# A hybrid encoder step: the order and banks of the last output stage, its last tile in halves, and a wait of the recurrence's tanh

## The reference

```
layer 0:  h = rms_norm(x) * (1 + scale) + shift;  u = h @ w_in        (x_a, g_a, q, k, v, g_b)
          y_a = rg_lru(conv(x_a)) * silu(g_a)     # r, i = sigmoid(xc @ w_a), sigmoid(xc @ w_x)
          y_b = window_attention(q, k, v) * silu(g_b)
          x = x + gate * rms_norm([y_a, y_b] @ w_out)
layer 1:  h = ...;  u = h @ w_in;  q, k, v = silu(conv(.));  gated delta rule over 8 heads
          x = x + gate * rms_norm((rms_norm(o) * silu(z)) @ w_out)    # the last stage
```

## Time and profile before

| | us |
|---|---|
| median of 3 runs (lowest, highest) | 1477.13 (1476.96, 1477.85) |
| the profiled execution | 1476.26 |
| its span, first to last instruction | 1474.5 |
| TensorE busy | 1418.5 (96%) |
| VectorE busy | 760.1 (52%) |
| ScalarE busy | 409.0 (28%) |
| GpSimd busy | 174.4 (12%) |
| TensorE's granted clock, mean share of full speed | 0.995 |

### The profile page before, as it was taken

How to read it: one execution, slowest core, us unless ns; L and a number is a source line. 1 busy time by engine, 2 the same in 40 slices (tenths; PEclk the granted TensorE clock), 3 DMA queues, 4 the chain that set the end, 5 groups by cost and what they waited for, 6 DMA issues and landing times.

```text
span 1474.5 us, 29798 instructions
## 1 busy us (share of the span) xinstructions
PE 1418.5 (96%) x12752; PEld 891.1 (60%) x12752; DVE 760.1 (52%) x1765; ACT 409.0 (28%) x1009; POOL 174.4 (12%) x341
## 2 busy tenths in 40 slices
PE   5999999999999999899999999999999999999997
PEld 3577765666644545566666666666666666665533
DVE  4737872444332444745747557465474574742252
ACT  5124431444411324112213123132221321322110
POOL 1122200000000110110201112011020020100120
PEclk9999999999999999999999999999999999999999
DMA  9520016000256011210111111101111011030151
GB/s 372 205 67 4 33 64 249 0 1 0 104 198 237 36 57 24 77 33 31 47 47 43 35 40 52 44 33 48 32 60 34 29 47 33 22 135 1 45 171 57
DMA packets 54439, 105.02 MB, mean 71 GB/s; under 512 B 34490, under 2 KB 37378, under 8 KB 51474
## 3 DMA queue, kind: packets, MB, share of 16 engines
q1 hardware_dynamic: 54308, 103.13, 20.2%
HBM read 88.25 MB, written 14.86 MB: 70 GB/s over the span
## 4 chain that ended last, share of the span: by engine, by line
PE 63%; DVE 6%; issue 1%; ACT 1%; DMA 0%; POOL 0%; POOLq 0%; DVEq 0%; ACTq 0%; SPq 0%
PE psum L787 61%; PE psum L790 2%; DVE mem L2228 1%; DVE mem L2245 1%; DVE mem L2460 1%; DVE mem L2259 1%; ACT mem L1644 0%; DVE mem L2397 0%; DVE mem L2238 0%; DVE mem L2406 0%; DVE mem L2142 0%; DMA mem<-eg_dram 0%; DVE mem L2148 0%; DVE mem L2225 0%; ACT mem L1610 0%
## 5 line engine op out<-in xcount | busy, mean ns | idle before, releaser
L787 PE MATMUL psum<-mem 32*32 32x32 f32 (+12 forms) x12144 | 1354.8, 297 | 32.1 <-issue 7.5
L787 PEld LDWEIGHTS psum<-mem 32*32 32x32 f32 (+4 forms) x12144 | 822.1, 137 | 525.5 <-issue 228.9
L2228 DVE SCALAR_TENSOR_TENSOR mem<-mem 128x384 f32<-128x384 f32 (+1 forms) x216 | 134.5, 623 | 2.7
L790 PE MATMUL psum<-mem 128*128 128x128 f32 (+1 forms) x608 | 86.0, 280 | 16.1 <-ACT mem L1439 11.1
L790 PEld LDWEIGHTS psum<-mem 128*128 128x128 f32 (+1 forms) x608 | 71.4, 145 | 49.2 <-issue 31.0
L2142 DVE SCALAR_TENSOR_TENSOR mem<-psum,mem 128x1024 f32<-128x1024 f32 x13 | 16.5, 1271 | 73.5 <-POOL mem L678 71.3
L1580 ACT ACTIVATE mem<-psum 128x1024 f32<-128x1024 f32 x13 | 13.3, 1024 | 127.9 <-PE psum L787 126.1
L1559 ACT ACTIVATE mem<-mem 128x256 f32<-128x256 f32 x72 | 35.5, 494 | 46.4 <-DVE mem L2102 46.4
L676 POOL TENSOR_SCALAR mem<-mem 128x1 f32<-128x1 f32 x18 | 5.8, 321 | 353.9 <-ACT mem L1580 353.9
L1709 ACT ACTIVATE mem<-mem 128x128 f32<-128x128 f32 x72 | 22.1, 307 | 81.9 <-DVE mem L2447 56.2
L2426 DVE COPY mem<-psum 128x128 f32<-128x128 f32 x64 | 18.7, 291 | 50.2 <-PE psum L787 49.8
(11 more groups left out here) (213 smaller groups left out, 1001.1 us busy)
## 6 DMA issues: line engine op xcount, KB each, us to landing
mem<-modw SPq DMA_DIRECT2D x12, 2048.0 KB, 12.3
mem<-w SPq DMA_DIRECT2D x44, 512.0 KB, 3.3
mem<-x SPq DMA_DIRECT2D x1, 4608.0 KB, 18.2
x_dram<-mem SPq DMA_DIRECT2D x9, 512.0 KB, 2.6
mem<-row_dram SPq DMA_DIRECT2D x8, 576.0 KB, 3.8
mem<-x_dram SPq DMA_DIRECT2D x9, 512.0 KB, 3.6
y<-mem SPq DMA_DIRECT2D x9, 512.0 KB, 3.6
mem<-wout SPq DMA_DIRECT2D x4, 1024.0 KB, 8.5
```

Source lines behind the costliest of these rows:

```text
L787: return pe.matmul(*a, **k)
L790: return pe.transpose(out, in_, ident[0:n, 0:n])
L2228: x = dve.scalar_tensor_tensor(cvm, U1[:, m, lo + j:hi + j], w, cvm, ALU.mult, ALU.add)
```

## The change

- **Order and banks of the last stage.** `OUT_ORDER` is 0, 1, 4, 2, 5, 3, 6, 8, 7: late tiles 4, 5 and 6 come between early ones. `OUT_BANK` gives each turn one of three bank pairs (0, 4 or 2). TensorE waits for `out_ev` of the last turn that used its pair, or of turn 0. VectorE issues the partial sum of an early tile that follows a late one behind the late one's `out`. Residual loads and outputs follow the new order.
- **The last tile by halves.** The last turn (tile 7) signals `out_mm` after each 512 columns. ScalarE squares each half by itself; GpSimd makes two scale operations, the second adding to the first, and then the power; VectorE multiplies each half by the gate right after its square, and later by the norm factor with the residual's addition in one operation for each half; SP sends two halves of 256 KB.
- **The recurrence.** Before tanh 0 of group m ScalarE waits for `l_a` of group m - 1, its own earlier result; the wait for `l_y` stands before tanh 3.

```
+OUT_ORDER = (0, 1, 4, 2, 5, 3, 6, 8, 7)
+OUT_BANK = (0, 4, 2, 0, 4, 0, 2, 0, 4)
 SP
-            for i, t in enumerate(EARLY + LATE):
-                if i < NT - 1:
-                    residual(i + 1)
+            for i, t in enumerate(OUT_ORDER[:-1]):
+                residual(i + 1)
                 sp.wait_ge(sem("x1_done"), NT + i + 1)
                 sp.dma_start(O["y"][:, t], XT[:, i % 2]).then_inc(sem(f"y_out{i % 2}"), 16)
+            for n in range(2):
+                half = slice(n * 512, n * 512 + 512)
+                sp.wait_ge(sem("x1_done"), 2 * NT + n)
+                sp.dma_start(O["y"][:, OUT_ORDER[-1], half], XT[:, 0, half]).then_inc(sem("y_out0"), 16)
 GpSimd
+            wait(pool, sem("o_ss"), 2 * NT)
+            c.mark(pool.tensor_scalar(stat[:, 9:10], stat[:, 6:7], 1.0 / D, EPS, ALU.mult, ALU.add))
+            wait(pool, sem("o_ss"), 2 * NT + 1)
+            c.sync()
+            c.mark(pool.tensor_scalar(stat[:, 9:10], stat[:, 7:8], 1.0 / D, stat[:, 9:10],
+                                      ALU.mult, ALU.add))
+            c.sync()
+            pool.tensor_tensor(stat[:, 10:11], stat[:, 9:10], halfneg[:, 0:1], ALU.pow
+                               ).then_inc(sem("o_rs"), 1)
 TensorE
-                    pe.wait_ge(sem("out_ev"), NT + i - 1)
+                    held = max([j for j in range(i) if OUT_BANK[j] == OUT_BANK[i]], default=0)
+                    pe.wait_ge(sem("out_ev"), NT + held + 1)
-                        x = mm(B(4 * (i % 2) + n), YT[:, k, t * P:(t + 1) * P],
+                        x = mm(B(OUT_BANK[i] + n), YT[:, k, t * P:(t + 1) * P],
-                x.then_inc(sem("out_mm"), 1)
+                    if n == 1 or i == NT - 1:
+                        x.then_inc(sem("out_mm"), 1)
-                    for i, t in enumerate(EARLY):
-                        out1(i, t, (KT - 1,))
-                    for i, t in enumerate(LATE):
-                        out1(len(EARLY) + i, t, range(KT))
+                    for i, t in enumerate(OUT_ORDER):
+                        out1(i, t, (KT - 1,) if t in EARLY else range(KT))
 ScalarE
                     if m and i == 0:
+                        wait(act, sem("l_a"), m)
+                    elif m and i == 3:
                         wait(act, sem("l_y"), m)
+            wait(act, sem("x1_done"), 2 * NT - 2)
+            for n in range(2):
+                wait(act, sem("out_mm"), 2 * NT + n)
+                wait(act, sem("o_ss"), 2 * NT - 1 + n)
+                act.activation(oj1[:, 0:512], B(OUT_BANK[-1] + n), ACT.Square, accum_out=stat[:, 6 + n:7 + n]
+                               ).then_inc(sem("o_ss"), 1)
 VectorE
-            for i, t in enumerate(EARLY + LATE):
-                if i + 1 < len(EARLY):
+            for i, t in enumerate(OUT_ORDER[:-1]):
+                early = t in EARLY
+                if early and OUT_ORDER[i + 1] in EARLY:
                     partial(i + 1)
                 dve.wait_ge(sem(f"xt_in{i % 2}"), 16 * (i // 2) + 16)
                 out(NT + i, i % 2, t == NT - 1, src, XT[:, i % 2], otmp1, not early)
+                if not early and OUT_ORDER[i + 1] in EARLY:
+                    partial(i + 1)
+            dve.wait_ge(sem("x1_done"), 2 * NT - 1)
+            halves = [slice(n * 512, n * 512 + 512) for n in range(2)]
+            for n, half in enumerate(halves):
+                dve.wait_ge(sem("o_ss"), 2 * NT + n)
+                c.mark(dve.tensor_tensor(otmp1[:, half], B(OUT_BANK[-1] + n), gate[:, 0, half], ALU.mult))
+            dve.wait_ge(sem("xt_in0"), 16 * 5)
+            dve.wait_ge(sem("o_rs"), 2 * NT)
+            c.sync()
+            for n, half in enumerate(halves):
+                dve.scalar_tensor_tensor(XT[:, 0, half], otmp1[:, half], stat[:, 10:11], XT[:, 0, half],
+                                         ALU.mult, ALU.add).then_inc(sem("x1_done"), 1)
```

More of the change, by code:

```diff
@@ L138 @@
 FIRST = 4
+OUT_ORDER = (0, 1, 4, 2, 5, 3, 6, 8, 7)
+OUT_BANK = (0, 4, 2, 0, 4, 0, 2, 0, 4)
+assert sorted(OUT_ORDER) == sorted(EARLY + LATE) and [t for t in OUT_ORDER if t in EARLY] == list(EARLY)
 def shares(p):
@@ L597, in residual @@
                     sp.wait_ge(sem(f"y_out{i % 2}"), 16 * (i // 2))
-                sp.dma_start(XT[:, i % 2], x1_dram[:, (EARLY + LATE)[i]]).then_inc(sem(f"xt_in{i % 2}"), 16)
+                sp.dma_start(XT[:, i % 2], x1_dram[:, OUT_ORDER[i]]).then_inc(sem(f"xt_in{i % 2}"), 16)
             head(H - 1, 0)
@@ L603, in _ @@
             residual(0)
[L604 to L606 removed]
+            for i, t in enumerate(OUT_ORDER[:-1]):
+                residual(i + 1)
                 sp.wait_ge(sem("x1_done"), NT + i + 1)
                 sp.dma_start(O["y"][:, t], XT[:, i % 2]).then_inc(sem(f"y_out{i % 2}"), 16)
[L609 removed]
+            for n in range(2):
+                half = slice(n * 512, n * 512 + 512)
+                sp.wait_ge(sem("x1_done"), 2 * NT + n)
+                sp.dma_start(O["y"][:, OUT_ORDER[-1], half], XT[:, 0, half]).then_inc(sem("y_out0"), 16)
+            sp.wait_ge(sem("y_out0"), 16 * 6)
             sp.wait_ge(sem("y_out1"), 16 * 4)
@@ L779, in _ @@
             head(H - 1, False)
-            for i in range(NT):
+            for i in range(NT - 1):
                 out_stats(NT + i, i % 2)
+            wait(pool, sem("o_ss"), 2 * NT)
[7 more added lines that the diff above has]
+                               ).then_inc(sem("o_rs"), 1)
         @block.tensor
@@ L1783, in _ @@
                     wait(act, sem("out_mm"), NT + i + 1)
-                    out(NT + i, i % 2, psum[:, 4 * (i % 2):4 * (i % 2) + 2], oj1)
+                    out(NT + i, i % 2, psum[:, OUT_BANK[i]:OUT_BANK[i] + 2], oj1)
+            wait(act, sem("x1_done"), 2 * NT - 2)
[4 more added lines that the diff above has]
+                               ).then_inc(sem("o_ss"), 1)
         @block.vector
@@ L2509, in partial @@
             def partial(i):
-                t = EARLY[i]
+                t = OUT_ORDER[i]
                 dve.wait_ge(sem("out_mm"), NT + i + 1)
@@ L2515, in partial @@
                 p = PART[:, t].rearrange("p (a d) -> p a d", a=2)
-                b = psum[:, 4 * (i % 2):4 * (i % 2) + 2]
+                b = psum[:, OUT_BANK[i]:OUT_BANK[i] + 2]
                 dve.tensor_tensor(p, p, b, ALU.add).then_inc(sem("out_ev"), 1)
@@ L2520, in _ @@
             partial(0)
-            for i, t in enumerate(EARLY + LATE):
-                if i + 1 < len(EARLY):
+            for i, t in enumerate(OUT_ORDER[:-1]):
+                early = t in EARLY
+                if early and OUT_ORDER[i + 1] in EARLY:
                     partial(i + 1)
                 dve.wait_ge(sem(f"xt_in{i % 2}"), 16 * (i // 2) + 16)
-                early = t in EARLY
                 src = (PART[:, t].rearrange("p (a d) -> p a d", a=2) if early
-                       else psum[:, 4 * (i % 2):4 * (i % 2) + 2])
+                       else psum[:, OUT_BANK[i]:OUT_BANK[i] + 2])
                 out(NT + i, i % 2, t == NT - 1, src, XT[:, i % 2], otmp1, not early)
+                if not early and OUT_ORDER[i + 1] in EARLY:
[11 more added lines that the diff above has]
+                                         ALU.mult, ALU.add).then_inc(sem("x1_done"), 1)
 def _rows(w):
```

## The result

| executions | us |
|---|---|
| after, median of 4 (lowest, highest) | 1467.01 (1465.77, 1468.28) |
| before on the same chip, median of 4 | 1477.49 (1476.96, 1479.07) |
| ratio after / before, 95% interval | 0.9918 [0.9901, 0.9936] |
| the profiled execution after, its span | 1466.97, 1465.2 |

The change makes the kernel 0.8% faster. The forecast was 0.6%, 8.8 us. The two medians of the table differ by 10.5 us, which would be 1466.7, just inside the range. The two profiled spans differ by 9.3 us. Every step named ahead shows in the new trace.

A forecast was written before the change was run, and what follows sets the result against it. TensorE, busy 96% of the span, was taken as the bound. 4.15 + 2.26 + 2.4 = 8.8 us off the profiled 1476.26 gave 1467.5, as a median of runs 1468.3 (-0.6%); range 1466.6 to 1471.4.

The forecast's parts named there:

- Part 1: Last stage: new order and third bank pair leave TensorE no hole between matmuls, 4.15 us won.
- The holes sum to 4.15 us: Last stage: TensorE's waits before late tiles, beyond the early records' 8.63 of 12.78 us, all to be won.
- Part 2: Tail after TensorE's last matmul: working the last tile by halves wins 2.26 us.
- 1.42 for 1.30: Tail: VectorE's last two operations, 512 columns each, were forecast at 1.30 us together, 1.24 less than before.
- The bounds of -1.2 and -3.1: Tail: least and greatest change in us that the forecast allowed around its sum of -2.26.
- Rival B: Tail gives less: multiplication uncovered or blocking GpSimd (0.7 us), output DMA gaining nothing (0.6); 1469.6 us, chance 0.14.
- the 0.6: Tail: us saved because the last output DMA carries 256 KB, not 512; taken between 0 and 1.3.
- Part 3: Recurrence: tanh 0 no longer waits for l_y in heads 1 and 2, winning 0.44 and 1.93, together 2.4 us.
- Rival A: Recurrence gives nothing because the pairs' adds on VectorE swallow the gain; 1470.7 us, chance 0.12.
- C: Last stage slower: TensorE waits 4.0 us three times for chained VectorE sums, if residuals are over 9.5 late; 1480.3, chance 0.03.
- D: Whole change: other waits replace each won piece, time within 1.5 us of before, 1476.5 us; chance 0.07.
- The base: Whole kernel: starting time before the change, 1477.13 us, the median of the runs shown.

The follow-up runs named there:

- again: The kernel before, unchanged, timed against itself and traced once more: ratio 0.9993.
- again0: The kernel before, unchanged, one more trace; no timed ratio given, its last stage's matmuls took 69.96 us against 67.99 in the first trace.
- recur: The kernel before with only the recurrence's waits moved (l_a before tanh 0, l_y before tanh 3): ratio 0.9980.
- halves: The kernel before with only the last tile by halves; order, bank pairs and recurrence as before: ratio 0.9996.
- gap: The kernel before, but turns 3 and 4 of the last stage each wait for one partial sum more: ratio 1.0019.
- thirds: The whole change with the last tile in 512, 256 and 256 columns on three banks, output in 704 and 320, third bank awaited before the turn: 0.9945.
- late: The whole change, but from turn 2 on SP loads a residual only after the output right before has landed: ratio 0.9967 to the kernel before.
- pairs2: The whole change with the new order but only two alternating bank pairs (0, 4): ratio 0.9970 to the kernel before.
- full: The whole change, unaltered, measured a second time against the kernel before: 1468.78 us, ratio 0.9929.
- full2: The whole change, unaltered, measured a third time against the kernel before, on the chip of again: 1467.93 us, ratio 0.9913.
- banksonly: The kernel before with three bank pairs in rotation and nothing else; old order, whole last tile, old recurrence wait: ratio 0.9969.

## Why the prediction was right and where it went wrong

**Part 1, TensorE's waits: the mechanism held, the size did not.** The step that failed is "The holes sum to 4.15 us", taken as all that the holes cost. It rests on one trace with the clock at 1.00 behind both waits. The holes are 4.15 us indeed (4.18 measured). But of six traces with the old order on two pairs and these waits (before, again, again0, recur, halves, and gap, where they are longer), five show the granted clock at half behind the first of them. It costs 0 in recur, 0.2 us in halves, 2.2 in again, 2.0 in again0, and in gap a share that can't be told from its longer waits. The remaining one, before, is the trace that the forecast had. Without gap the mean is 0.9 us. None of the twelve traces with the new order or a third pair shows it. The forecast's sum has no term for the clock, and its range left only 1.7 us for any gain above the forecast.

**Part 2, the tail:** right to 0.13 us in the traces. Only its smallest terms missed: 1.42 for 1.30, and 0.27 for 0.19. The 0.27 is not the multiplication's doing: the scale with constants took 0.19 beside the same multiplication in thirds. The bounds of -1.2 and -3.1 don't follow from the terms, which give -1.0 and -3.0. Rival B did not happen: GpSimd's power took 0.54, its first half beside the multiplication. (The row that the forecast leaned on, 0.55 at 1403.44, was weaker than it looked: VectorE's L2517 was over after its first 0.18 us.) GpSimd's first scale of this tile did get caught, at no cost. Its row and the row of VectorE beside it:

```profile
1453.47 1.27 POOL L789 TENSOR_SCALAR mem<-mem 128x1 f32<-128x1 f32 x1 [1.45 <-ACT mem L1806]
...
1453.47 1.22 DVE L2171 TENSOR_TENSOR mem<-mem 128x1024 f32<-128x1024 f32 x1
```

It took 1.27 us instead of 0.19 while VectorE added two SBUF operands. By the rule of the Trainium skill, "SBUF — State Buffer", section "Who interferes with whom", an operation with two SBUF operands takes the shared port and one that reads PSUM and SBUF leaves it free; the 1.27 here and the 0.54 of the power agree. The Trainium skill, "DMA: Bandwidth & Descriptors", section on the anatomy of one DMA, gave 0.60 us for half the bytes, by a sum that it states for DMAs of GpSimd's path; SP issues these, and 0.58 was measured. From the rows alone the 0.6 was luck. Its straight line starts from 3.6 us for 512 KB out, the median of one trace; in again, again0 and after it is 2.6, and a line to that would have given 0.2.

**Part 3, the recurrence:** 2.58 for 2.4, and 0.3 us of margin at tanh 3 for 0.4. The tanhs of groups 1 and 2 came 0.55 and 2.03 us earlier for 0.44 and 1.93. Rival A is refuted: R is 94.87 in all nine traces that have the wait at tanh 3, M is not longer for it, and recur is faster by itself. Here too the clock was left out: in two of eight traces with the old wait it fell behind the 2.06 us hole and took 1.39 us, 0.35 us in the mean. It fell in none of the others.

**Rivals C and D:** C's trigger was not reached even in late, where every residual from turn 3 on is waited for. Where TensorE does wait for a late tile's eviction (pairs2), it costs 1.85 us three times, not 4.0. D is refuted by every row above.

**The sum.** The traces give 8.89 us, and the clock behind the removed waits 0.9 + 0.35 more: 10.1. Timed, the change brought 12.1, 10.5 and 12.9 us in three comparisons, each with an interval of 2.1 to 2.7 either way, so 11.8 in the mean, with some 1.4 either way. The 8.9 of the parts is too little for that, and 10.1 still falls a little short.

The granted clock of the executions looks at the account from another side. Over all 229 executions under 2000 us, of all kernels, a straight line with one level for each kernel gives 1.14 us for each 0.001 of mean clock; it explains six tenths of the variance within a kernel. Executions of before have 0.9914 in the mean (95 of them), those of the whole change 0.9944 (14): 3.4 us. At equal clock the line leaves 8.2 us (interval 1.1) for after and full together and 9.2 (1.6) for full2, so it agrees with the 8.89 of the traces. The line compares; it does not prove a cause.

Not all of the 3.4 is time won. The mean clock also counts the tail, in which TensorE does nothing, and there the clock falls too. The windows of the tail, before and after:

```profile
1466.65:1474.50 7.85, 0.00 (x0) 0.00 (x0) 2.51 (x2) 1.11 (x2) 0.73 (x2) 0.80 0.16 67
```

```profile
1459.48:1465.20 5.72, 0.00 (x1) 0.00 (x0) 2.11 (x3) 0.69 (x2) 0.81 (x2) 0.97 0.24 92
```

That is 3.1 us at half clock before and 0.3 after. The mean is 3.8 over the seven traces with a tail of 7.8 us and 1.9 over the ten with one under 6. A difference of 1.9 us at half clock is 0.0006 to 0.0007 of the mean clock, so some 0.7 us of the 3.4 by the line. It costs nothing: T is 7.85 at a clock of 0.80 in before and 7.87 at 0.74 in banksonly.

How much of the rest comes from the removed waits stays open: 1.2 us are located in the traces. banksonly, which changes nothing but most of the last stage's waits, has 0.9921 where the 23 executions of before on its chip have 0.9911. The difference, 0.0010 with an interval of 0.0011, is 1.1 us by the line: it fits the 0.9 located there and leaves little for more. What remains, some 1.5 us, may be chance in which executions were profiled, or falls elsewhere that the change doesn't touch.

The base was off as well: 1477.13 was the median of three executions, while 95 have a mean of 1479.9.

## What to carry to other kernels

A hole in TensorE's row costs its own length and, in some executions, the clock behind it. A fallen clock in a stretch in which TensorE is idle costs nothing, so a mean clock is no price. Before a sum rests on one trace, compare the same records in several: equal counts with longer times are a fallen clock. When a stage waits for banks, look for an unused pair first, since here it closed six sevenths of the holes and the reordering the rest, and the reordering without it made things worse. A wait moved to the last place that needs it can be free with 0.3 us to spare: it is worth finding the row in which the result arrives.

## What the hardware showed that I had not expected

- With one and the same code, a wait of 2.05 us ahead of 4 records and a second wait was followed by half clock in two traces (again, again0) and not in the third (before). It also was in recur and halves, which leave that stretch as it is, and in gap, where the wait was 3.77. Three waits of 1.85 us with 15.72 us of matmuls between them (pairs2) were not, nor one of 1.94 (thirds). The single wait of 2.06 in the recurrence was, in two traces of eight.
- Where the clock falls, the next wait can hide it: in recur the clock was 0.68 from 1406 to 1411, and the second wait vanished: the last 132 records stand in one piece of 58.80 us, and S stayed at 67.99. In again0 that wait shrank from 1.60 to 0.53.
- Where nothing was changed, the clock also falls, and over all executions the mean clock goes with six tenths of the scatter. TensorE's row of after ahead of such a place, and its window:

```profile
1017.47 7.72 PE L802 MATMUL psum<-mem 32*32 32x64 f32 x73 [1.85 <-issue]
```

```profile
1015.00:1022.00 7.00, 5.15 (x76) 3.60 (x65) 1.22 (x4) 0.32 (x1) 0.00 (x0) 0.76 0.04 5
```

- Below 512 KB the size hardly matters for an output. From issue to landing 64 KB took 2.3 us, 160 and 352 KB 2.2 and 2.3 (thirds), 256 KB 2.0 and 512 KB 2.6 (after).
